# MLA attention scores as three products of rounded halves instead of one fp32 product

## The reference

```python
q = (rmsnorm_2(cq, g) @ w_uq).reshape(B, L, 16, 64 + 32)      # 64 plain and 32 rotary columns
kv = (rmsnorm_2(ckv, g) @ w_ukv).reshape(B, L, 16, 64 + 64)
q_m = concat([q_nope, rope(q_pe, pos)])                       # each head its own
k_m = concat([k_nope, k_pe])                                  # k_pe is one for all heads
s = einsum('bhqd,bhkd->bhqk', q_m, k_m) / sqrt(96)            # causal
p = softmax(s);  o = p @ v
```

## Time and profile before

| | |
|---|---|
| median of 3 runs | 1472.34 us (1472.07 to 1472.43) |
| the profiled execution | 1473.41 us, its span 1471.6 us |
| PE busy | 1451.9 us (99%) |
| DVE busy | 828.5 us (56%) |
| ACT busy | 691.1 us (47%) |
| POOL busy | 161.6 us (11%) |
| MLA attention, round 0 to round 17 | about 837 to 957 us of the span |

### The profile page before, as it was taken

One profiled execution on the slowest core, in us unless ns is written; L12 is line 12 of the kernel. 1 busy time (PEld: TensorE's weight loads), 2 busy tenths in 40 slices (PEclk: granted clock), 3 DMA queues, 4 the chain that ended last, 5 costly groups with the idle time before them and its releaser, 6 DMA issues.

```text
span 1471.6 us, 26477 instructions
## 1 busy us (share of the span) xinstructions
PE 1451.9 (99%) x11311; PEld 1284.0 (87%) x11311; DVE 828.5 (56%) x1335; ACT 691.1 (47%) x1025; POOL 161.6 (11%) x308
## 2 busy tenths in 40 slices
PE   7999999999999999999999999999999999999998
PEld 7999989999999898998888777788899888778888
DVE  6487867764656556654335787642223566644343
ACT  6475877853443222322233676642222777743232
POOL 0025400000000000000000044300000233320000
PEclk9999999999999999999999999999999999999999
DMA  7222121123422223222334333433223333342222
GB/s 238 94 66 89 63 83 59 59 73 137 131 94 86 87 87 113 87 87 82 106 101 108 63 47 20 77 94 109 86 86 89 68 71 71 72 105 93 86 94 79
DMA packets 138968, 130.24 MB, mean 89 GB/s; under 512 B 26569, under 2 KB 134884, under 8 KB 138596
## 3 DMA queue, kind: packets, MB, share of 16 engines
q1 hardware_dynamic: 134084, 120.39, 26.0%
q0 software_dynamic: 4752, 8.16, 5.3%
q10 hardware_dynamic: 16, 0.00, 0.0%
HBM read 119.69 MB, written 4.26 MB: 84 GB/s over the span
## 4 chain that ended last, share of the span: by engine, by line
PE 91%; DVE 3%; ACT 3%; issue 1%; DMA 0%; SPq 0%; DVEq 0%; ACTq 0%
PE PS L962 79%; PE PS L1288 3%; PE PS L1261 2%; PE PS L1244 2%; DVE wlo L1937 1%; PE PS L1248 1%; PE PS L1247 1%; PE PS L1073 1%; ACT L1439 1%; ACT whi L1439 0%; DMA xt<-in_x 0%; ACT Pm L1439 0%; PE PS L1129 0%; PE PS L1029 0%; DVE zlo L1985 0%
## 5 line engine op out<-in xcount | busy, mean ns | idle before, releaser
L962 PE MATMUL PS<-zhi,whi 128*128 128x258 f32 (+2 forms) x1856 | 486.9, 320 | 3.2 <-ACT qf L1439 1.0
L962 PE MATMUL PS<-zhi,wlo 128*128 128x258 f32 (+2 forms) x1856 | 476.8, 314 | 0.0
L962 PE MATMUL PS<-zlo,whi 128*128 128x258 f32 (+2 forms) x1856 | 475.4, 314 | 0.6 <-DVE zlo L1985 0.6
L962 PEld LDWEIGHTS PS<-zhi,whi 128*128 128x128 f32 x1856 | 306.9, 189 | 27.9 <-issue 2.6
L962 PEld LDWEIGHTS PS<-zhi,wlo 128*128 128x128 f32 x1856 | 305.6, 189 | 22.3
L962 PEld LDWEIGHTS PS<-zlo,whi 128*128 128x128 f32 x1856 | 305.5, 189 | 20.8 <-DVE zlo L1985 0.8
L1937 DVE TENSOR_TENSOR wlo<-raw,whi 128x2048 fp32r<-128x2048 f32 (+2 forms) x114 | 249.3, 2187 | 121.5 <-ACT whi L1439 121.4
L1439 ACT ACTIVATE whi<-raw 128x2048 fp32r<-128x2048 f32 (+2 forms) x114 | 207.4, 1820 | 150.4 <-DMA raw<-in_w_up 55.2
L1439 ACT ACTIVATE Pm<-Pm,small 128x144 f32<-128x144 f32 (+3 forms) x128 | 73.1, 571 | 38.6 <-DVE small L2467 38.3
L2467 DVE CUSTOM_DVE_ANT_0 Pm<-PS,cmask 128x144 f32<-128x144 f32 (+3 forms) x128 | 62.9, 503 | 35.8 <-PE PS L1244 21.5
L962 PE MATMUL PS<-glo,whi 128*128 128x512 f32 x176 | 69.9, 397 | 0.0
(11 more groups left out here) (357 smaller groups left out, 2171.4 us busy)
## 6 DMA issues: line engine op xcount, KB each, us to landing
raw<-in_w_in SPq DMA_DIRECT2D x50, 1024.0 KB, 5.3
raw<-in_w_up SPq DMA_DIRECT2D x22, 1024.0 KB, 5.1
raw<-in_w_out SPq DMA_DIRECT2D x8, 1024.0 KB, 5.2
raw<-in_w_down SPq DMA_DIRECT2D x8, 1024.0 KB, 5.3
raw<-in_w_br_mla SPq DMA_DIRECT2D x4, 1024.0 KB, 5.1
raw<-in_w_br_fox SPq DMA_DIRECT2D x4, 1024.0 KB, 5.1
raw<-in_w_down SPq DMA_DIRECT2D x4, 768.0 KB, 4.3
hspill<-hT SPq DMA_DIRECT2D x1, 2112.0 KB, 7.6
```

The lines of the kernel that those rows point to most:

```text
L962: ins = mm(o_, l_, r_, start=first, stop=last)
```

## The change

The scores of MLA are made as hi*hi + hi*lo + lo*hi in fp32r, from `qhi`, `qlo`, `khi` and `klo`. Four engines share the halves:

- VectorE writes the scaled query to `qsum` where it wrote `qh`. ScalarE rounds it to `qhi` (`q_high`, 128x512, for head h+1 in the hook `ahead` of round h, between the exponential of block 1 and the copy of turn group 0). GpSimd makes `qlo` (`query_low`, 128x512, after its copy of block 1), and scores(h, 0) wait for it.
- ScalarE's `k_out` writes `khi` and no longer frees the accumulator. VectorE makes `klo` from the same accumulator (`k_low`, two operations of 64x264) and frees it. It does so in the next round, after `mla_project` and before the maximum of block 0.
- The rotary rows of the keys, one set for all heads: VectorE makes one sum and two low halves, ScalarE two high halves, GpSimd copies them for other heads (`rope_rows` in rounds 0, 3 and 11) where VectorE made copies at the start.
- `klo` of some heads lies in the places of weight units. So the loads of three units wait for scores: the second half of `w_uq` for those of heads 0 to 3, two units of the next stage for heads 0 to 11 and for all 16. `MZ_AT` becomes rounds 5, 13, 16 and 17: VectorE's `w_low` now stands in rounds 6 and 14, in round 17 and after the loop.
- Semaphores are merged, and some tiles placed anew, with no other work in it.

```diff
-        MZ_AT = {2: (pl.uq[1],), 10: (U(("mz", 0)),), 15: (U(("mz", 2)),), 16: (U(("mz", 4)),)}
+        MZ_AT = {5: (pl.uq[1],), 13: (U(("mz", 0)),), 16: (U(("mz", 2)),), 17: (U(("mz", 4)),)}
...
+            SCORES_READ = {pl.uq[1]: 4, U(("mz", 0)): 12, U(("mz", 2)): HEADS}
...
+                if u in SCORES_READ:
+                    sp.wait_ge(mla.s_done, 4 * SCORES_READ[u])
...
+            def query_low(x):
+
+                pool.wait_ge(q_hi, x + 1)
+                nc.gpsimd.tensor_tensor(qlo[x % 2][:, :], qsum[x % 2][:, :], qhi[x % 2][:, :].bitcast(F32), ALU.subtract)\
+                  .then_inc(q_lo, 1)
...
+                        pe.wait_ge(q_lo, h + 1)
...
+                if A is mla:
+                    for x, (lhs, rhs) in enumerate(((qhi[h % 2], khi[h % 4]), (qhi[h % 2], klo[h]), (qlo[h % 2], khi[h % 4]))):
+                        for dst, c0 in cuts:
+                            c1 = c0 + dst.shape[-1]
+                            ins = mm(dst, lhs[:, t0:t0 + P], rhs[:, c0:c1], start=x == 0, stop=x == 2)
...
-                    if A is mla:
-                        ins = mm(dst, qh[h % 2][:, t0:t0 + P], kh[h % 4][:, c0:c1], start=True, stop=True)
...
-                tick(A_(kh[2 * x % 4][0:NOPE, cols], acc_real(n, slice(0, NOPE), HALF), ACT.Copy))
-                tile_free(A_(kh[2 * x % 4 + 1][0:NOPE, cols], acc_real(n, slice(NOPE, P), HALF), ACT.Copy), n)
+                for r in range(2):
+                    A_(khi[2 * x % 4 + r][0:NOPE, cols], acc_real(n, slice(NOPE * r, NOPE * (r + 1)), HALF), ACT.Copy)\
+                        .then_inc(k_hi, 1)
+
+            def q_high(x):
+                tile_freed(act, ("mq", x))
+                A_(qhi[x % 2][:, :], qsum[x % 2][:, :], ACT.Copy).then_inc(q_hi, 1)
...
-            attention(mla, mla_project, lambda h: None, mla_after)
+            attention(mla, mla_project, lambda h: q_high(h + 1) if h < HEADS - 1 else None, mla_after)
...
+            def attention(A, project, between, ahead, after):
                 for h in range(HEADS + 2):
                     project(h)
+                    if h:
+                        after(h - 1)
                     for i in range(4):
...
+            def k_low(x, b):
+                n, cols = ("mk", x, b), slice(HALF * b, HALF * (b + 1))
+                dve.wait_ge(k_hi, 4 * x + 2 * b + 2)
+                if x >= 2:
+                    dve.wait_ge(mla.s_done, 8 * (x - 1))
+                for r in range(2):
+                    ins = V.tensor_tensor(klo[2 * x + r][0:NOPE, cols], acc_real(n, slice(NOPE * r, NOPE * (r + 1)), HALF),
+                                          khi[2 * x % 4 + r][0:NOPE, cols].bitcast(F32), ALU.subtract)
+                    if r == 0:
+                        tick(ins)
+                tile_free(ins, n)
+
+            def mla_after(h):
+                if h < HEADS - 2:
+                    k_low(h // 2 + 1, h % 2)
```

More of the change, by code:

```diff
@@ L430, in build_program @@
         e += 2 * 1344 * 4
-        PT = [at(f"PT{i}", [P, 14 * P], F32, e + i * 14 * P * 4)[0] for i in range(2)]
-        Pe = [at(f"Pe{i}", [P, P], F32, e + (i + 1) * 14 * P * 4 - P * 4)[0] for i in range(2)]
+        PT = [at(f"PT{i}", [P, 1344], F32, e + i * 1344 * 4)[0] for i in range(2)]
+        Pe = [at(f"Pe{i}", [P, P], F32, e + (26 + i) * P * 4)[0] for i in range(2)]
         e += 2 * 14 * P * 4
@@ L833, in move_ends, with rope_rows @@
                     nc.gpsimd.dma_start(vtok[32 * i:32 * i + NM, QB, :], vtok[0:NM, i + 1, :]).then_inc(A.v_moved, 16)
+            def rope_rows(h):
+                done = {0: K_LOW, 3: K_SECOND, 11: K_FOURTH}[h]
+                pool.wait_ge(mla.e_ready, 4 * h + 3)
+                pool.wait_ge(q_lo, h + 2)
+                pairs = [(dst, klo_a[1]) for dst in (klo_b if h == 3 else klo_c)]
+                if h == 0:
+                    pool.wait_ge(kr_step, K_LOW)
+                    pairs = [(khi[2], khi[0]), (khi[3], khi[0])] + pairs
+                else:
+                    tile_done(pool, ("mq", h + 1))
+                for n, (dst, src) in enumerate(pairs):
+                    nc.gpsimd.tensor_copy(dst[64:P, :], src[64:P, :]).then_inc(kr_step, 1)
+                    pool.wait_ge(kr_step, done + n + 1)
+            def query_low(x):
+                pool.wait_ge(q_hi, x + 1)
+                nc.gpsimd.tensor_tensor(qlo[x % 2][:, :], qsum[x % 2][:, :], qhi[x % 2][:, :].bitcast(F32), ALU.subtract)\
+                  .then_inc(q_lo, 1)
             def gather_ends(A):
@@ L854, in gather_ends @@
                     for i in range(QB):
+                        if A is mla and i == 2 and h + 1 < HEADS:
+                            query_low(h + 1)
+                        if A is mla and i == 3 and h in (0, 3, 11):
+                            rope_rows(h)
                         pool.wait_ge(A.p_exp, 4 * h + i + 1)
@@ L865, in _ @@
             pool.wait_ge(e_cleared, 2)
+            query_low(0)
             gather_ends(mla)
@@ L1724, in _ @@
             w_high(pl.uq[0])
+            act.wait_ge(kr_step, K_SUM)
+            for i in range(2):
+                A_(khi[i][64:P, :], PT[0][64:P, 0:T], ACT.Copy).then_inc(kr_step, 1)
             tile_freed(act, ("cq", 1))
@@ L1788, in mla_project @@
                     k_out(0, 1)
+                    q_high(0)
                 if h == 1:
@@ L2455, in _ @@
             v_out(4, 1)
-            def attention(A, project, between, ahead):
+            V.tensor_tensor(klo_a[0][r_, :], t1, khi[0][r_, :].bitcast(F32), ALU.subtract).then_inc(kr_step, 1)
+            def attention(A, project, between, ahead, after):
                 for h in range(HEADS + 2):
                     project(h)
+                    if h:
+                        after(h - 1)
                     for i in range(4):
```

80 lines of the change are left out of this document (48 added, 32 removed).

## The result

The changed kernel takes 1501.93 us (1500.89 to 1503.66, 4 runs) and the kernel before 1472.38 us (1472.07 to 1472.75, 4 runs): a ratio of 1.0202 [1.0189, 1.0215]. The forecast was 1486, in a range that ended at 1491. The sign was right, the size less than half of what came (14 us for 29). One of the four executions of the kernel of experiment 5 was slow, 1529.31 us at a mean granted clock of 0.90, and is left out of what is said of that kernel; with it its median is 1495.08.

What follows compares the result with a forecast made beforehand. TensorE was taken as the bound, with even rounds to wait for VectorE's key release. Start 3.3, rounds 4, 8, 10, 12 4 x 1.52, round 6 3.1, round 14 3.0, odd rounds -7 x 0.27: +13.6 us, 1486; range 1480 to 1491.

Steps and rivals of the forecast that it cites:

- the release of the keys: Even rounds: TensorE's first scores wait until VectorE's `k_low` frees the key block; round 7.41 us long, 1.52 more than before.
- Behind them come 0.72, 0.54 and 0.73 of scores, 0.37 of keys and 1.65 of residual and turns: Even rounds, TensorE's work after the key wait: 4.01 us in all.
- the term of the even rounds: Rounds 4, 8, 10 and 12: four times 1.52 us more, 6.1 us.
- The start: First query's halves pass over ScalarE and GpSimd: first scores at 839.3, 2.0 us later; 3.3 late through round 2.
- In round 2 ... the keys at 852.2: Round 2: next query done at 851.5, keys at 852.2, round ending at 856.3 instead of 853.01, 3.3 us late.
- `k_low`: VectorE's two 64x264 operations from PSUM: 0.70 us for both, with 0.45 and 1.20 as ends.
- TensorE's saving: Scores as three fp32r products: 0.27 us saved in an odd round, 0.48 in an even one.
- the rival in which TensorE stays the bound: All MLA rounds keep the score saving, 5.3 us less, with 2.0 lost at the start: 1469 us; chance 0.06.
- Round 6: `w_low` moved into this even round on VectorE: it ends at 9.0 us, 3.1 more than before.
- the late load of `w_uq`: Load starting with round 3's last scores, wanted in round 5 10.6 us later: takes 8.2 us, hidden; at worst some 5 late.
- The rival in which GpSimd and VectorE block each other: Each even round 1.1 us longer, or `w_uq` up to 5 us late: 1490 to 1494 us; shared chance 0.12.
- The rival "ScalarE is the bound": Keys freed soon enough by VectorE, ScalarE's copies set even rounds at 6.8 us: 1481 us in all; chance 0.12.

Runs made afterwards that it cites:

- experiment 5: Changed kernel with VectorE's `k_low` moved behind the maximum of block 3 of the round that made the block, for every head: 1494.58 us, 3 runs.
- experiment 4: Changed kernel with the key block made in an odd round read by ScalarE and VectorE in that same round: 1486.59 us.
- Experiment 1: Changed kernel with seven useless matmuls on TensorE in front of its key wait in each even round: 1493.11 us.
- experiment 2: Changed kernel with TensorE's wait for the rotary low half moved from ahead of the first query projection to the first scores: 1498.59 us.
- experiment 3: Kernel before with three fp32r products of the same operands in place of the fp32 scores, no low halves: 1469.33 us.
- experiments 9 and 10: Changed kernel, `k_low` in the making round, low keys, low query or both cut to 8 columns (1489.39, 1491.63, 1484.09 us); then without low key piece (1477.45 us).
- experiment 11: Changed kernel with start, `k_low` and small pieces moved, `w_low` in even rounds, ScalarE's high key half ahead of the exponentials of blocks 2 and 3: 1483.77 us.
- experiment 8: Changed kernel with start, `k_low` and `w_low` moved, `q_high` behind the copy of turn group 0, z piece behind the maximum of block 1: 1488.32 us.
- first kernel of experiment 9: Changed kernel with `k_low` in the round that made the block and the low key pieces cut to 8 of 264 columns: 1489.39 us.

## Why the prediction was wrong

*Right: the release of the keys decides.* `scores(h, 0)` of each even round waits for VectorE's `k_low`. Round 2 came out at 7.42 for 7.41, but with luck in it: round 1 has no product with the row sums, and the scores start at 3.16 for 3.4, while what comes behind takes 4.29 for 4.01 (chain of waits). A kernel that releases them earlier without more work in the round (experiment 4) has even rounds of 5.6 to 6.0.

*Failed: "Behind them come 0.72, 0.54 and 0.73 of scores, 0.37 of keys and 1.65 of residual and turns".* This step took what comes behind the wait at the length that it has in an unbroken row. Behind a wait of some 2 us TensorE ran at half clock in five of the six even rounds from 4 on, and at the start, and the same pieces took 1.6 us more (3.98 for 2.38). Experiment 1, which fills the wait, has no half clock and is 6.6 us shorter in rounds 4 to 12, of which some 0.5 is the DMA of round 10, and 1.5 shorter at the start. This is the largest part of the 14 us missed. Half of the 14 is in the term of the even rounds (13.05 for 6.1). Even at full clock the first scores behind a wait take 0.95 and not the 0.71 of the unbroken row.

*Failed: "The start".* It was forecast at 2.0 for the first scores and came at 6.2. I followed the query through ScalarE and GpSimd, but took the rotary low half as a small delay of the accumulators (0.4). TensorE's own wait for it stood ahead of the first query projection: 2.42 of idle, and half clock on the projections behind it. Moving that wait brings the first scores to 839.40 (experiment 2), and the forecast's own chain over ScalarE and GpSimd had 839.3. "In round 2 ... the keys at 852.2" then came late by the same amount. A wait in round 1 (1.78), where the accumulator of the keys was still held for `k_low`, was not foreseen, but the round is only 0.65 longer than before, near the 0.5 that the forecast gave it for another reason.

*Mis-sized: `k_low`*, 0.88 for 0.70, inside its bounds. With the hand-over of 0.24 to TensorE the scores start 0.14 later than forecast, and what comes behind takes some 0.27 more, nearly all of it in the first scores: a round without half clock is 7.8 to 7.9 instead of 7.4.

*Mis-sized: TensorE's saving.* The pieces came as priced from FOX (0.71, 0.55 and 0.73), but an odd round got only 0.16 shorter, not 0.27. By experiment 3 the whole is worth 2.95, not 5.3, and the rival in which TensorE stays the bound was not reached by any full version.

*Right: the other terms.* Round 6 took 4.05 more for a forecast of 3.1; at full clock, in experiment 1, it took 3.3 more (9.18). The half clock costs less there than elsewhere, since part of it runs beside `w_low`: turn 3 waits 0.24 for VectorE with it and 1.18 without. Further, the late load of `w_uq` was hidden (ScalarE does not idle before its `w_high` in round 5); GpSimd's low query half is on the path of the changed kernel at the start only. The rival in which GpSimd and VectorE block each other did not come: the z pieces took 0.68 to 0.80, not above 1.

*The rival "ScalarE is the bound"* forecast 6.8 for the even rounds once VectorE frees the keys soon enough. With `k_low` early they took 7.29, and 6.75 with it short. By experiments 9 and 10 it is the wait of VectorE for ScalarE's high half and the low pieces themselves that make the difference, since with neither the rounds take 5.9 to 6.0 with `q_high` still in ScalarE's row. Between the changed kernel and experiment 11, 18.2 us came back by order alone; how the last 11 above the kernel before split between VectorE's 0.88 a round, `w_low` and the start was not taken apart further.

## What to carry to other kernels

Where a change makes TensorE wait, price the idle time and then what follows it: look in the rows behind the wait for the granted clock, and in a forecast, add a second case in which the work behind it runs at half clock. Where a split moves work from TensorE to the engines that hand it its operands, their mean load (VectorE 56%) says little: count the hand-overs inside a round, and ask for each new piece which engine's result it waits for and what is queued behind it. Experiments 9 and 10 are the check: first cut the piece's columns and keep its place, then take it out. Read in the timeline how long the short piece still is (two of 8 columns took 0.36 here, for 0.88) before you put the rest down to the wait.

## What was not expected of the hardware

- TensorE's granted clock falls to 0.50 after idle times of 2.05 to 2.75 us in an otherwise full row, in round 4 from 872.3 to 875.7, and not in every execution: it did after 2.22 us in round 4 of the kernel after and did not after 2.21 in the same round of experiment 2, and at the start it did after 2.42 us and did not after 2.43 in experiment 1. Nor does it take one long wait: in the kernel of experiment 8 it fell at about 840.7, when TensorE was busy again for 1.9 us behind a wait of 1.76, and in the first kernel of experiment 9 at about 950.8, behind waits of 0.66, 0.62 and 0.26.
- GpSimd's subtraction of 128x512 takes 1.26 to 1.30 us, where its product of 543 columns took 1.09; and two copies of 16 columns again took as long as the `w_low` that it ran beside (2.26 and 2.23 us).
